# Moving operands that begin at remainders of 32 to 448 bytes modulo 512, weights left at 0

## The reference

```python
def swiglu(h, w_in, w_out):
    gate, up = jnp.split(h @ w_in, 2, axis=-1)
    return (jax.nn.silu(gate) * up) @ w_out

def first_block(...):
    x = x + 0.5 * swiglu(rms_norm(x, norm_ffn1_w[l]), ffn1_w_in[l], ffn1_w_out[l])
    x = x + hybrid_mixer(rms_norm(x, norm_mix_w[l]), ...)
    x = x + memory_cross_attention(rms_norm(x, norm_cross_w[l]), rms_norm(mem, norm_mem_w[l]), ...)
    x = x + 0.5 * swiglu(rms_norm(x, norm_ffn2_w[l]), ffn2_w_in[l], ffn2_w_out[l])
```

## Time and profile before

| what | value |
|---|---|
| median of three runs | 2134.65 us (2134.08 to 2134.89) |
| span of the profiled execution, first to last instruction | 2133.4 us |
| median less that span | 1.25 us |
| PE busy, matmuls | 2114.8 us, 99% of the span, 10122 matmuls |
| PE busy, weight loads (beside the matmuls) | 1740.7 us, 10122 loads |
| DVE, ACT, POOL busy | 829.8, 803.6, 1120.5 us |
| bytes moved | 207.7 MB, 97 GB/s mean |

### The profile page before, as it was taken

One profiled execution on the slowest core, in us unless ns is written; L12 is line 12 of the kernel. 1 busy time (PEld: TensorE's weight loads), 2 busy tenths in 40 slices (PEclk: granted clock), 3 DMA queues, 4 the chain that ended last, 5 costly groups with the idle time before them and its releaser, 6 DMA issues.

```text
span 2133.4 us, 29164 instructions
## 1 busy us (share of the span) xinstructions
PE 2114.8 (99%) x10122; PEld 1740.7 (82%) x10122; DVE 829.8 (39%) x1489; ACT 803.6 (38%) x1345; POOL 1120.5 (53%) x1493
## 2 busy tenths in 40 slices
PE   9999999999999999999999999999999999999999
PEld 7888888878887778877888888887787888888887
DVE  5222211762841766143322222208744474023244
ACT  5222232325834655323322223326554343122233
POOL 6555555673354337725655555554545466555554
PEclk9999999999999999999999999999999999999999
DMA  6322233233322213412332223321222223332322
GB/s 214 119 98 98 99 106 106 85 99 96 114 99 79 75 55 122 155 40 89 99 98 98 95 94 117 99 96 63 79 89 79 89 80 108 99 99 99 99 89 80
DMA packets 61344, 207.71 MB, mean 97 GB/s; under 512 B 6616, under 2 KB 8088, under 8 KB 61256
## 3 DMA queue, kind: packets, MB, share of 16 engines
q1 hardware_dynamic: 55216, 195.84, 27.8%
q10 hardware_dynamic: 6040, 10.65, 1.5%
HBM read 204.31 MB, written 4.77 MB: 98 GB/s over the span
## 4 chain that ended last, share of the span: by engine, by line
PE 42%; issue 28%; POOL 27%; DVE 2%; POOLq 0%; ACT 0%; DMA 0%; SPq 0%; DVEq 0%; ACTq 0%
POOL w_lo L463 27%; PE bank L516 11%; PE bank L518 11%; PE bank L517 11%; PE bank L678 1%; PE bank L680 1%; PE bank L679 1%; PE bank L908 1%; PE bank L932 1%; PE bank L840 1%; PE bank L920 0%; DVE gx_lo L2394 0%; DVE bank L2403 0%; PE bank L846 0%; DVE x L2405 0%
## 5 line engine op out<-in xcount | busy, mean ns | idle before, releaser
L463 POOL TENSOR_TENSOR w_lo<-w_raw,w_hi 128x256 fp32r<-128x256 f32 x1448 | 1087.1, 783 | 933.4 <-ACT w_hi L1283 933.3
L516 PE MATMUL bank<-gx_hi,w_hi 128*128 128x512 f32 (+1 forms) x1768 | 674.9, 382 | 7.8 <-DVE gx_lo L2394 4.5
L518 PE MATMUL bank<-gx_hi,w_lo 128*128 128x512 f32 (+1 forms) x1768 | 668.1, 378 | 0.0
L517 PE MATMUL bank<-gx_lo,w_hi 128*128 128x512 f32 (+1 forms) x1768 | 667.6, 378 | 0.0
L1283 ACT CAST w_hi<-w_raw 128x1024 fp32r<-128x1024 f32 x364 | 378.4, 1045 | 347.9 <-PE bank L518 291.8
L516 PEld LDWEIGHTS bank<-gx_hi,w_hi 128*128 128x128 f32 x1768 | 332.6, 188 | 74.2 <-DVE gx_lo L2394 6.4
L518 PEld LDWEIGHTS bank<-gx_hi,w_lo 128*128 128x128 f32 x1768 | 332.5, 188 | 62.1
L517 PEld LDWEIGHTS bank<-gx_lo,w_hi 128*128 128x128 f32 x1768 | 332.7, 188 | 60.5 <-issue 0.2
L516 PE MATMUL bank<-ff_hi,w_hi 128*128 128x512 f32 x352 | 136.9, 389 | 0.0
L517 PE MATMUL bank<-ff_lo,w_hi 128*128 128x512 f32 x352 | 136.9, 389 | 0.0
L518 PE MATMUL bank<-ff_hi,w_lo 128*128 128x512 f32 x352 | 136.9, 389 | 0.0
(11 more groups left out here) (358 smaller groups left out, 2703.4 us busy)
## 6 DMA issues: line engine op xcount, KB each, us to landing
w_raw<-wstream SPq DMA_DIRECT2D x364, 512.0 KB, 3.5
bias_spread<-bias_rows ACTq DMA_DIRECT2D x1, 2560.0 KB
square<-cum_rows ACTq DMA_DIRECT2D x8, 256.0 KB, 3.5
rfin_row<-cum_rows ACTq DMA_DIRECT2D x8, 256.0 KB, 3.1
outT<-ple_o SPq DMA_DIRECT2D x8, 256.0 KB, 2.0
x<-xT SPq DMA_DIRECT2D x3, 512.0 KB, 8.0
square<-bias_spread ACTq DMA_DIRECT2D x4, 256.0 KB, 2.6
rfin_row<-bias_spread ACTq DMA_DIRECT2D x4, 256.0 KB, 2.7
```

Source lines behind the costliest of these rows:

```text
L463: ins = nc.gpsimd.tensor_tensor(w_lo[:, s, part], w_raw[:, s, part], w_hi[:, s, part].bitcast(F32), ALU.subtract)
L516: nc.tensor.matmul(dst, hi, rhs[0], start=first, stop=False)
L517: nc.tensor.matmul(dst, hi, rhs[1], start=False, stop=False)
L518: return nc.tensor.matmul(dst, lo, rhs[0], start=False, stop=last)
```

## The change

Eight pairs of operand tiles begin so many bytes behind a multiple of 512 in each partition: `gx` 128, `ff` 256, `ys` 32, `o` 192, `ox` 320, `cv` 384, `o2` 448, `up` 96. `p` stays at 0 and `m` at 64; the slots `w_raw`, `w_hi`, `w_lo` stay at 0. Chunks are 2048 bytes as before, so every chunk of a tile has its tile's remainder. For tiles in the region to have room for the shift, each 8 KB of it is followed by a gap of 512 bytes, and `REGION` is now a multiple of 2048. The room comes from the scratch that is set aside at the start of SBUF for DMA descriptors, 16 KB before and 1 KB now. `prob`, `w_T`, `o_nrm` and small tiles that lie inside `gx` move with it.

```diff
+GAP = 512
+SHIFT = {"gx": 128, "ff": 256, "ys": 32, "o": 192, "ox": 320, "cv": 384, "o2": 448, "up": 96}
...
-        cursor[0] = -(-cursor[0] // LINE) * LINE
+        cursor[0] = -(-cursor[0] // LINE) * LINE + SHIFT["gx"]
         GX_HI, GX_LO = cursor[0], cursor[0] + DC * S * 4
         gx_hi = fixed("gx_hi", [DC, S], F32R)
         gx_lo = fixed("gx_lo", [DC, S], F32R)
+        cursor[0] = -(-cursor[0] // LINE) * LINE
         w_raw = fixed("w_raw", [RING, UNIT])
...
-        REGION = -(-cursor[0] // 512) * 512
-        cursor[0] = REGION + 96 * 1024 + 64
+        REGION = -(-cursor[0] // LINE) * LINE
+        cursor[0] = REGION + 96 * 1024 + 12 * GAP + 512
...
-        def at(name, kb, shape, dt=F32):
-            off = REGION + int(kb * 1024)
+        def at(name, kb, shape, dt=F32, shift=0):
+            off = REGION + int(kb * 1024) + int(kb // 8) * GAP + shift
...
-        ff_hi = at("ff_hi", 0, [FC, S], F32R)
-        ff_lo = at("ff_lo", 44, [FC, S], F32R)
+        ff_hi = at("ff_hi", 0, [FC, S], F32R, shift=SHIFT["ff"])
+        ff_lo = at("ff_lo", 44, [FC, S], F32R, shift=SHIFT["ff"])
...
-    nc = bacc.Bacc("TRN2", target_bir_lowering=False, num_devices=1)
+    nc = bacc.Bacc("TRN2", target_bir_lowering=False, num_devices=1, dynamic_dma_scratch_size=1024)
```

More of the change, by code:

```diff
@@ L257, in build @@
         ysq_tmp = at("ysq_tmp", 69, [GH * SHD])
-        ys_hi = at("ys_hi", 16, [DC, S], F32R)
-        ys_lo = at("ys_lo", 32, [DC, S], F32R)
+        ys_hi = at("ys_hi", 16, [DC, S], F32R, shift=SHIFT["ys"])
+        ys_lo = at("ys_lo", 32, [DC, S], F32R, shift=SHIFT["ys"])
         q_T = at("q_T", 48, [AH, S])
@@ L307, in build @@
         bias_h = [square, rfin_row]
-        o_hi = at("o_hi", 48, [AH, S], F32R)
-        o_lo = at("o_lo", 64, [AH, S], F32R)
+        o_hi = at("o_hi", 48, [AH, S], F32R, shift=SHIFT["o"])
+        o_lo = at("o_lo", 64, [AH, S], F32R, shift=SHIFT["o"])
         load_sq = at("load_sq", 0, [DC, S])
@@ L324, in build @@
         qx_T = at("qx_T", 48, [DC, S])
-        ox_hi = at("ox_hi", 64, [DC, S], F32R)
-        ox_lo = at("ox_lo", 80, [DC, S], F32R)
+        ox_hi = at("ox_hi", 64, [DC, S], F32R, shift=SHIFT["ox"])
+        ox_lo = at("ox_lo", 80, [DC, S], F32R, shift=SHIFT["ox"])
         m_sum = at("m_sum", 40.0625, [ML])
@@ L333, in build @@
         v2_tok = at("v2_tok", 16, [TT, S])
-        cv_hi = at("cv_hi", 24, [4, S], F32R)
-        cv_lo = at("cv_lo", 32, [4, S], F32R)
+        cv_hi = at("cv_hi", 24, [4, S], F32R, shift=SHIFT["cv"])
+        cv_lo = at("cv_lo", 32, [4, S], F32R, shift=SHIFT["cv"])
         gates = at("gates", 40, [16, S])
-        o2_hi = at("o2_hi", 0, [4, S], F32R)
-        o2_lo = at("o2_lo", 8, [4, S], F32R)
+        o2_hi = at("o2_hi", 0, [4, S], F32R, shift=SHIFT["o2"])
+        o2_lo = at("o2_lo", 8, [4, S], F32R, shift=SHIFT["o2"])
         cc_t = at("cc_t", 64, [S])
@@ L366, in build @@
         post_sum = rfin_row
-        up_hi = at("up_hi", 16, [HC, S], F32R)
-        up_lo = at("up_lo", 48, [HC, S], F32R)
+        up_hi = at("up_hi", 16, [HC, S], F32R, shift=SHIFT["up"])
+        up_lo = at("up_lo", 48, [HC, S], F32R, shift=SHIFT["up"])
         f_acc = at("f_acc", 80, [DC, S])
```

## The result

The changed kernel takes 2168.32 us (2167.61 to 2168.4, four runs) against 2134.77 us for the kernel before (four runs as well): 33.5 us slower, or 1.0155 times as long, 95% interval 1.0141 to 1.017. The profiled execution has a span of 2166.6 us against 2133.4.

The account below looks back on a forecast made before the run. PE was taken as the bound: the number of matmuls times each one's pitch in a stream. The terms summed to -6.2 us, from a span of 2133.4 to 2127.2, so a median of 2128.4 us; range 2092 to 2180.

Parts of the forecast that it names:

- each matmul of either length pays 13.3 ns on top: On PE: 512 columns take 213.3 ns at one column per cycle; the extra 13.3 ns is all an address can touch.
- 64 ahead saves a little and 64 behind costs three times as much: Stages using m: moving at +64, 256 columns, -2.2 ns; stationary, distance -64, 512 columns, +6.7 ns.
- Term 1: Products with gx moving at 128: 5400 matmuls at -2.2 ns each, -11.9 us.
- Term 2: up at 96 and o at 192: 1056 matmuls at -2.2 ns, -2.3 us; ys at 32: -0.2 us.
- Term 3: ff at 256: 1056 matmuls at +2.25 ns, the middle of -2.2 and +6.7, +2.4 us.
- Term 4: ox at 320, cv at 384, o2 at 448: 384 matmuls at +6.7 ns, +2.6 us.
- Term 5: Stationary gx at 128 under moving weights at 0: 480 matmuls, priced as distance -64, +3.2 us.
- Terms 6 to 8: Unmoved p and m, other engines' accesses to shifted tiles, smaller DMA scratch and gaps: all costed at nothing.
- The settled state is lost: Rival, chance 0.34: shifted moving operands stay at 232.2 ns, not 226.7; 2182 us for all, 2170 if only gx.

Follow-up runs that it names:

- e8: All eight shifted operand tiles and the weights w_hi, w_lo at 128, against the kernel before the change: 2134.39 us against 2135.29, ratio 0.9995.
- e10: Only gx shifted, to 64, against the kernel before the change: 2146.59 us, ratio 1.0052.
- e4: The map: separate kernel, not the reference's work, streams of 72 products with both operands at chosen remainders; 512 columns: 226.7 ns at distance 0, 229.0 at 64.
- e1: The changed kernel with all eight shifts at 0, its gaps, region base and small scratch kept: 2135.46 us, ratio 0.9996 against the kernel before.
- e5: Separate kernel, not the reference's work: streams as in e4 with fewer weight columns, other moving lengths and other data types; bfloat16 took 215.8 ns per product.

## Why the prediction was wrong

*What bounds the kernel.* Right: PE, through the pitch. The same chain now costs more per matmul, with nothing else changed. That "each matmul of either length pays 13.3 ns on top" is right for distance 0 alone: 256 columns at distance 192 pay 6.6 (113.3 less 106.7).

*What the trace shows of addresses.* The two pitches were read rightly. What was made of them, "64 ahead saves a little and 64 behind costs three times as much", was not: the two places differed in direction and in length at once, and it was the length that turned a saving into a cost. With 256 columns 64 behind saves too (the keys of e8, at distance 192: 113.4), and with 512 columns 64 ahead costs (e10). e8 and the map bear out that the distance counts, and that zero effect (the rule of "SBUF — State Buffer", section "Who interferes with whom", in the Trainium skill: TensorE never waits for anyone) is not what these runs show for rounded float32. For bfloat16 and plain float32 they agree with it: no distance tried changed the pitch. The period was taken to be 512 bytes; it is 256.

*Term 1, moving `gx` at 128: the step that failed.* I gave it -2.2 ns, "the nearest distance measured, +64", 5400 times, -11.9 us. That step carried a saving measured at 256 columns over to 512 columns because the 13.3 ns at distance 0 are alike for both. At other distances they are not alike: at 64 the effect is -2.2 ns with 256 columns and +2.2 with 512 (e4, e10), and at 128 it is -1.4 and +5.7 or more. The term measured +26.4 us for the 512-column products and -0.4 for the halves. The trace of the kernel before held no row for a moving operand off 0 with 512 columns; the only 512-column row off 0 was the +6.7, and by that one the term would have been a loss.

*Term 2, `up`, `o`, `ys`:* forecast -2.5 us, measured +4.5 for `up`, +0.3 for `ys` and +1.1 for `o`. The same step failed.

*Term 3, `ff` at 256:* forecast +2.4, measured 0.0. Wrong by the period.

*Term 4, `ox`, `cv`, `o2`:* forecast +2.6 (1.3, 0.6 and 0.6); measured +0.3, +0.4 and +0.2. `ox` at 320 is at 64 modulo 256, where the map has 2.2 ns and not 6.7. `cv` and `o2` took 231.6 and 232.3 ns where they had 226.7 in their unbroken pieces; a part of that was made up by shorter waits inside the two groups.

*Term 5, stationary `gx`:* forecast +3.2, measured +2.2. The sign and the price were right where the stream is unbroken: 233.3 ns from 1426 us on, where 233.4 was expected. In the earlier stages with `gx` stationary other work breaks the stream, and they had stood at 228.2 ns on average (steps under 260 ns) and not at 226.7; they went to 232.5. So the forecast is 1.4 times what was measured.

*Terms 6 to 8:* right. `m` stayed at 117.8 and 233.3 and `p` cost nothing, the other engines' new addresses and the small scratch cost nothing (e1).

*The rivals.* "The settled state is lost", at 0.34, gave the direction and the size: 232.2 ns from the nine steps behind a break, where `gx` now has 232.4 and 233.3, and 2170 us if only `gx` did it (2182 for all), where the time was 2168.3. Its mechanism is borne out in part. The 226.7 is lost at the shifted tiles with 512 columns, but other distances settle too, each at pitches of its own, and `ff` at 256 kept 226.7. And the 2170 is near by some luck: it took `gx` at +29.7 and the rest at +5.7, where they measured +26.0 and +9.0. The range, 2092 to 2180, held the time. The direction was forecast wrongly, and what stands above under term 1 is why.

One thing stays open: what happens in PE or SBUF at a meeting of the two streams. The runs show that of the three forms tried only the rounded 4-byte one has it, that it depends on the distance of the two addresses modulo 256 and on the number of columns of both operands, and that a stream can settle at more than one pitch. They do not show a mechanism.

No version was found that is clearly faster. For 512 columns nothing on a grid of 32 bytes beat distance 0, and the 6.7 ns that 256-column streams can gain at distance 192 came in only some entries.

## What to carry to other kernels

In a stream of rounded float32 matmuls of 512 columns, put the weights and the moving operand at the same remainder modulo 256 bytes; which remainder it is does not matter. Any other distance that was tried for all three products alike cost 2 to 8 ns of 227 per matmul (11 at 4 bytes). For other lengths this is no rule: at 256 and 448 columns other distances were faster than 0, at 320 none mattered. Bfloat16 and plain float32 showed no such cost at 512 columns. A difference of pitch read at one length of the stream is no evidence for another length, and one long stream settled at a value is no evidence that the same stream always settles there: before a row is multiplied by 5400, ask in what it differs from the 5400.

## What the runs showed that I had not expected

- A stream's settled pitch depends on what ran before it, with operands and addresses the same: 113.3 or 117.8 ns for 256 columns at distance 192. Of the four distances, taken over both lengths, 0 is the only one that always came back to one value (226.7 and 120.0).
- With 512 columns rounded float32 pays 13.3 ns over its columns even at best, where bfloat16 pays 2.5 (215.8 ns).
- In e5 the granted clock stood at 0.50, the 1.2 GHz level, while streams of 64 and of 128 moving columns ran, although PE shows no idle time there. It fell within the first stream of 64 columns, behind 512-column streams at full clock, and came back in the first stream of 192 columns. This is one run. The stretches (columns as in the earlier trace rows):

```profile
391.00:400.00 9.00, 9.00 (x71) 0.86 0.01 2
...
478.00:560.00 82.00, 82.00 (x387) 0.50 0.00 1
...
570.00:580.00 10.00, 10.00 (x70) 0.75 0.01 2
```
